# Prompt-chunk filler matmuls of a hybrid decoder step: six of eight weight tiles as three products of rounded halves

## The reference

```python
h = rms_norm(x, norm_mix)
u = h @ w_in                                  # RWKV part, attention part (q, k, v, f), gates
o_r = rwkv_time_mix(u_r, ...)                 # a delta-rule state, scanned over the rows
o_f = attend(q, k, v, log_sigmoid(f + b))     # softmax attention with forget bias
merged = sigmoid(g_r) * (o_r @ w_br_rwkv) + sigmoid(g_f) * (o_f @ w_br_fox)
x = x + merged @ w_out
x = x + square(relu(rms_norm(x) @ w_ffn_up)) @ w_ffn_down
```

## Time and profile before

| | us |
|---|---|
| median of 3 runs | 2157.71 (2157.24 to 2160.13) |
| the profiled execution's own time | 2151.56 |
| its span, first to last instruction | 2149.6 |
| TensorE busy | 2072.9 (96%) |
| VectorE busy | 908.4 (42%) |
| ScalarE busy | 597.7 (28%) |
| GpSimd busy | 191.8 (9%) |
| first fillers to the end of chunk 9 | 221 to 854 |

### The profile page before, as it was taken

The page is one execution under the profiler, slowest core; times in us unless marked ns, Lnnn a source line. Parts: engine busy times, 40 slices in busy tenths (PEclk is TensorE's granted clock), DMA queues, the critical chain, the costliest instruction groups (busy, mean ns, idle before and its releaser), DMA issues.

```text
span 2149.6 us, 42585 instructions
## 1 busy us (share of the span) xinstructions
PE 2072.9 (96%) x17394; PEld 1795.7 (84%) x17394; DVE 908.4 (42%) x1468; ACT 597.7 (28%) x963; POOL 191.8 (9%) x186
## 2 busy tenths in 40 slices
PE   7999999999999999999999999999999999999997
PEld 7996677777777777655566899999999999999997
DVE  6557444433444442505776654432222213212334
ACT  5015222221222222213544642332012102202213
POOL 0000222122222212001110000000000000000000
PEclk9999999999999999999999999999999999999999
DMA  4204421101222111764745461111111111111112
GB/s 166 88 30 174 149 49 41 48 22 40 49 60 69 49 45 55 186 137 157 251 134 204 150 236 60 49 39 49 49 39 49 47 41 49 40 48 49 39 49 81
DMA packets 107238, 181.05 MB, mean 84 GB/s; under 512 B 60014, under 2 KB 63406, under 8 KB 105542
## 3 DMA queue, kind: packets, MB, share of 16 engines
q1 hardware_dynamic: 104806, 170.65, 25.2%
q10 hardware_dynamic: 2304, 8.50, 1.6%
HBM read 145.58 MB, written 33.54 MB: 83 GB/s over the span
## 4 chain that ended last, share of the span: by engine, by line
PE 70%; issue 17%; POOL 4%; DVE 3%; DMA 3%; SPq 1%; ACT 1%; POOLq 0%; ACTq 0%; DVEq 0%
PE ps L289 41%; PE ps L369 13%; PE ps L946 3%; POOL arena L2194 3%; PE ps L947 3%; DMA weights<-in_wu 1%; PE ps L1262 1%; DVE arena L1953 1%; PE ps L1128 1%; PE ps L1065 1%; PE ps L1187 1%; PE ps L1246 1%; DVE arena L1972 1%; DMA normed<-in_kp 1%; PE ps L1058 1%
## 5 line engine op out<-in xcount | busy, mean ns | idle before, releaser
L369 PE MATMUL ps<-normed,weights 128*128 128x350 f32 x1344 | 432.1, 469 | 0.8 <-ACT arena L382 0.6
L369 PEld LDWEIGHTS ps<-normed,weights 128*128 128x128 f32 x1344 | 246.6, 191 | 128.1 <-issue 7.3
L289 PE MATMUL ps<-h_high,wb_split 128*128 128x350 f32 x1536 | 290.5, 324 | 0.0
L289 PE MATMUL ps<-ff_high,wb_split 128*128 128x350 f32 x1488 | 281.0, 323 | 0.0
L299 ACT CAST wb_split<-weights 128x1024 fp32r<-128x1024 f32 x88 | 92.1, 1047 | 599.8 <-PE ps L289 591.9
L289 PEld LDWEIGHTS ps<-h_high,wb_split 128*128 128x128 f32 x1536 | 254.7, 189 | 0.4
L289 PEld LDWEIGHTS ps<-ff_high,wb_split 128*128 128x128 f32 x1488 | 247.2, 189 | 0.0
L2111 DVE TENSOR_TENSOR arena<-arena,ps 128x1050 f32 (+1 forms) x39 | 48.7, 1249 | 314.0 <-PE ps L289 314.0
L946 PEld LDWEIGHTS ps<-arena 64*64 64x64 f32 x2400 | 145.0, 135 | 26.5 <-issue 26.5
L2194 POOL TENSOR_TENSOR arena<-arena,constants 64x512 f32<-64x512 f32 x120 | 132.5, 1104 | 386.7 <-DVE arena L1803 325.2
L289 PE MATMUL ps<-ff_low,wb_split 128*128 128x350 f32 x744 | 160.3, 323 | 0.0
(11 more groups left out here) (305 smaller groups left out, 2863.4 us busy)
## 6 DMA issues: line engine op xcount, KB each, us to landing
weights<-in_wu SPq DMA_DIRECT2D x122, 512.0 KB, 3.5
normed<-in_vp SPq DMA_DIRECT2D x64, 260.0 KB, 4.4
normed<-in_kp SPq DMA_DIRECT2D x64, 256.0 KB, 5.3
arena<-chunk_dram SPq DMA_DIRECT2D x10, 1248.0 KB, 6.9
arena<-gate_dram SPq DMA_DIRECT2D x16, 525.0 KB, 4.0
chunk_dram<-arena SPq DMA_DIRECT2D x12, 520.0 KB, 5.3
chunk_dram<-fox SPq DMA_DIRECT2D x12, 520.0 KB, 4.6
arena<-samp_dram SPq DMA_DIRECT2D x10, 512.0 KB, 10.2
```

The lines of the kernel that those rows point to most:

```text
L289: last = pe.matmul(PS[:, 3 * s + g, 0:G], ws[s][wh][:, k * P:(k + 1) * P], tile_of(x[xh], k)[:, g * G:(g + 1) * G], start=(k == 0 and wh + ...
L369: last = self.pe.matmul(PS[:, 6 + m % 2, 0:G], W[:, s, k * P:(k + 1) * P], HT[:, k, g * G:(g + 1) * G], start=(k == 0), stop=(k == KT - 1))
```

## The change

The kernel's fillers of chunks 1 to 9 do the tiles k = 0 to 5 as three float32r products, the tiles 6 and 7 as before in float32. The order within a sub-unit becomes 6, 7, 0, ..., 5. For this:

- In chunk 0 ScalarE rounds six tiles of `HT` into `HF` (one behind each level's copies). After chunk 0 VectorE writes the low halves in place over the six tiles, `HL` (same memory as `HT`), 128x1050 each, and the first fillers of chunk 1 wait for them (`hl_made`). After chunk 9 it adds the halves back (`h_restored`); the first fillers after the chunks wait for that, and so does ScalarE before it writes `f_t`.
- The weights of a slot are split in each chunk: slot 1 in the chunk itself (ScalarE behind the copy `nat_k`, VectorE behind `nat_v`, ahead of the masks, in two parts of 512 and 256 columns), slot 0 of the next pair in the chunk before (ScalarE behind level 5, VectorE behind the levels). The low half is written in place over `W`.
- To make room, the low-rank gate goes to DRAM (`bg_dram` doubled, four more stores of 520 KB before chunk 0) and comes back with the bonus, so each chunk's load has twice the bytes; and four buffers share memory with others (`E2` with `Lm`, `NU` with `T1`, `Yc` with `Xm`; `gst` moves).
- Chunks 0 and 9 stand outside the loops of VectorE and ScalarE; otherwise the chunks are as before.

```diff
-                self.left = [(s, g, k) for s in range(2) for g in range(NG) for k in range(KT)]
+                late = [*range(NS, KT), *range(NS)] if ns or first else range(KT)
+                self.left = [(s, g, i, k) for s in range(2) for g in range(NG) for i, k in enumerate(late)]
...
+                        if g == 0 and self.ns:
+                            self.pe.wait_ge(wf_done[s], self.v - V_FOX0)
...
+                    if m == 0 and self.first is not None and k < NS:
+                        self.pe.wait_ge(self.first, k + 1)
+                    out, w = PS[:, 6 + m % 2, 0:G], W[:, s, k * P:(k + 1) * P]
+                    if k < self.ns:
+                        wl_ = WL[:, s, k * P:(k + 1) * P]
+                        self.pe.matmul(out, fill_w(s, k), HF[:, k, at], start=False, stop=False)
+                        self.pe.matmul(out, fill_w(s, k), HL[:, k, at], start=False, stop=False)
+                        last = self.pe.matmul(out, wl_, HF[:, k, at], start=False, stop=(i == KT - 1))
+                    else:
+                        last = self.pe.matmul(out, w, HT[:, k, at], start=(i == 0), stop=(i == KT - 1))
...
+        def fill_split_high(act, i, s):
+            act.wait_ge(w_in[s], 16 * i + 16 * (V_FOX0 + 1))
+            for k0, k1, t in WF[s]:
+                last = act.copy(t, W[:, s, k0 * P:k1 * P])
+            last.then_inc(wf_high[s], 1)
+        def fill_split_low(dve, i, s):
+            dve.wait_ge(wf_high[s], i)
+            for k0, k1, t in WF[s]:
+                last = dve.tensor_tensor(WL[:, s, k0 * P:k1 * P], W[:, s, k0 * P:k1 * P], t, ALU.subtract)
+            last.then_inc(wf_done[s], 1)
...
+            for p in range(HP):
+                sp.wait_ge(gt_read, NG * (p + 1))
+                sp.dma_start(bg_dram[:, HP + p, :], GT[:, p, 0:TP]).then_inc(bg_stored, 16)
...
-                fill = Filler(pe, c + V_FOX0) if c else fill0
+                fill = Filler(pe, c + V_FOX0, NS, hl_made if c == 1 else None) if c else fill0
...
-            Filler(pe, V_GATE0 + (NC - C_FOX)).run()
+            Filler(pe, V_GATE0 + (NC - C_FOX), first=h_restored).run()
...
                 ch_act.done(act.copy(Kn[0:C], PS[0:C, 0, :]), "nat_k")
+                if early:
+                    fill_split_high(act, c, 1)
...
+                    if lv == 5 and late:
+                        fill_split_high(act, c + 1, 0)
+                    if not early:
+                        if lv == 1:
+                            act.wait_ge(bg_stored, 16 * 2 * HP)
+                        act.copy(HF[:, lv - 1], HT[:, lv - 1, :]).then_inc(hf_made, 1)
...
+            act.wait_ge(h_restored, NS)
             order(act.activation(f_t[0:NH], lfT[0:NH], ACT.Abs))
...
                 done(dve.tensor_copy(Vn[0:C], PS[0:C, 3, :]), "nat_v")
+                if early:
+                    fill_split_low(dve, c, 1)
...
+                if late:
+                    fill_split_low(dve, c + 1, 0)
...
+            dve_chunk(0, early=False)
+            dve.wait_ge(hf_made, NS)
+            dve.wait_ge(unit_done, 2 * V_FOX0 + 2)
+            for k in range(NS):
+                dve.tensor_tensor(HL[:, k], HT[:, k, :], HF[:, k], ALU.subtract).then_inc(hl_made, 1)
+            with dve.Fori(1, NC - 1) as c:
+                dve_chunk(c)
+            dve_chunk(NC - 1, late=False)
+            dve.wait_ge(unit_done, 2 * (V_FOX0 + NC - 1) + 2)
+            for k in range(NS):
+                dve.tensor_tensor(HT[:, k, :], HL[:, k].bitcast(F32), HF[:, k].bitcast(F32), ALU.add)\
+                   .then_inc(h_restored, 1)
...
-                ch_pool.done(pool.tensor_tensor(here, here, GT[:, :, bass.ds(c * C, C)], ALU.mult), "gate")
+                ch_pool.done(pool.tensor_tensor(here, here, BGc[:, HP:2 * HP], ALU.mult), "gate")
```

More of the change, by code:

```diff
@@ L83 @@
 C_FOX = PV_FOX
+NS = 6
 SB_COLS = 56904
@@ L159, in build @@
         cst = keep_tensor("constants", C_ALL)
+        w_at = placed
         W = keep_tensor("weights", 2, D)
@@ L162, in build @@
         wl = keep_tensor("lora_weights", 512)
+        wg_at = placed
         wg = keep_tensor("gate_weights", 512)
@@ L354, in build, with __init__ @@
         class Filler:
-            def __init__(self, pe, v):
-                self.pe, self.v = pe, v
-                self.left = [(s, g, k) for s in range(2) for g in range(NG) for k in range(KT)]
+            def __init__(self, pe, v, ns=0, first=None):
+                self.pe, self.v, self.ns, self.first = pe, v, ns, first
+                late = [*range(NS, KT), *range(NS)] if ns or first else range(KT)
+                self.left = [(s, g, i, k) for s in range(2) for g in range(NG) for i, k in enumerate(late)]
             def run(self, n=None):
-                for s, g, k in self.left[:n]:
+                for s, g, i, k in self.left[:n]:
                     m = NG * s + g
-                    if k == 0:
-                        if g == 0:
+                    at = slice(g * G, (g + 1) * G)
+                    if i == 0:
+                        if g == 0 and self.ns:
+                            self.pe.wait_ge(wf_done[s], self.v - V_FOX0)
+                        elif g == 0:
                             self.pe.wait_ge(w_in[s], 16 * self.v + 16)
                         self.pe.wait_ge(sub_read, 2 * NG * self.v + (m + 1 - 2 * NG * V_FOX0))
-                    last = self.pe.matmul(PS[:, 6 + m % 2, 0:G], W[:, s, k * P:(k + 1) * P],
-                                          HT[:, k, g * G:(g + 1) * G], start=(k == 0), stop=(k == KT - 1))
-                    if k == KT - 1:
+                    if m == 0 and self.first is not None and k < NS:
[8 more added lines that the diff above has]
+                        last = self.pe.matmul(out, w, HT[:, k, at], start=(i == 0), stop=(i == KT - 1))
+                    if i == KT - 1:
                         last.then_inc(unit_done if g == NG - 1 else sub_done, 1)
@@ L520, in build @@
         Lc, Lm = r_ch.take(HP, C), r_ch.take(HP, C)
-        E1, E2, E3 = r_ch.take(HP, C), r_ch.take(HP, C), r_ch.take(HP, C)
+        E1, E2, E3 = r_ch.take(HP, C), Lm, r_ch.take(HP, C)
         AR = r_ch.take(HP, 2, C)
         Kc, Bc, Vc = r_ch.take(HP, C), r_ch.take(HP, C), r_ch.take(HP, C)
-        Kn, Bn, Vn = r_ch.take(512), r_ch.take(512), r_ch.take(512)
+        Kn, BGc, Bn, Vn = r_ch.take(512), r_ch.take(2 * HP, C), r_ch.take(512), r_ch.take(512)
         HB, HR = 64, C - 64
@@ L534, in build, with fill_w @@
         Zm = r_c2.take(512)
-        NU = r_c2.take(512)
+        NU = T1.rearrange("p a b -> p (a b)")
+        Yc = Xm.rearrange("p a b -> p (a b)")
+        gst = r_c2.take(4, NH)
         St = r_ch.take(HP, HD)
[L537 to L540, removed]
+        hf_at = -(-r_ch.at // 8) * 8
+        HF = own("fill_high", hf_at, NS, TT, dtype=F32R)
+        HL = own("fill_low", ht_at, KT, TT, dtype=F32R)
+        wf_at = hf_at + -(-NS * TT // 8) * 8
+        WF = [[(0, NS, own("w_fill0", wf_at, NS * P, dtype=F32R))],
+              [(0, 4, own("w_fill1a", wg_at, 4 * P, dtype=F32R)),
+               (4, NS, own("w_fill1b", wf_at + NS * P, (NS - 4) * P, dtype=F32R))]]
+        WL = own("w_fill_low", w_at, 2, D, dtype=F32R)
+        assert r_ch.at <= GT_at and wf_at + (2 * NS - 4) * P <= ar_end
+        wf_high, wf_done = [sem("wf_high0"), sem("wf_high1")], [sem("wf_done0"), sem("wf_done1")]
+        hf_made, hl_made, h_restored = sem("hf_made"), sem("hl_made"), sem("h_restored")
+        def fill_w(s, k):
+            return [t[:, (k - k0) * P:(k - k0 + 1) * P] for k0, k1, t in WF[s] if k0 <= k < k1][0]
+        def fill_split_high(act, i, s):
[8 more added lines that the diff above has]
+            last.then_inc(wf_done[s], 1)
         bonus_added = sem("bonus_added")
@@ L1441, in gate_out, with act_chunk @@
                 act_fill(act, x + V_GATE0, m, SGs[:, s, g * G:(g + 1) * G])
-            def act_chunk(c, gates):
+            def act_chunk(c, gates, early=True, late=True):
                 def out(m):
@@ L1504, in act_chunk @@
                                                bias=par[:, V_LB + p:V_LB + p + 1]), f"y_{p}")
-            with act.Fori(0, C_FOX) as c:
+            act_chunk(0, False, early=False)
+            with act.Fori(1, C_FOX) as c:
                 act_chunk(c, False)
-            with act.Fori(C_FOX, NC) as c:
+            with act.Fori(C_FOX, NC - 1) as c:
                 act_chunk(c, True)
+            act_chunk(NC - 1, True, late=False)
             act.wait_ge(ch_pe.sem, ch_pe.before(NC))
@@ L1773, in _, with dve_chunk @@
             dve.sem_inc(ch_dve.sem, 1)
-            with dve.Fori(0, NC) as c:
+            def dve_chunk(c, early=True, late=True):
                 def wait(steps, name):
@@ L2200, in _ @@
                 here = YT[:, :, bass.ds(c * C, C)]
-                ch_pool.done(pool.tensor_tensor(here, here, BGc, ALU.add), "bonus")
+                ch_pool.done(pool.tensor_tensor(here, here, BGc[:, 0:HP], ALU.add), "bonus")
```

(2 more changed lines are left out.)

4 lines of the change are left out of this document (2 added, 2 removed).

## The result

The changed kernel took 2140.2 us in the median of six executions (2131.3 to 2144.5), beside 2156.1 (2149.4 to 2160.1) of the kernel before; the ratio is 0.993, interval [0.9906, 0.9955]. The forecast was 2144.1, within 2134 to 2154. The gain of the medians is 15.8 us against 13.6 forecast.

A forecast was written before the change was run, and what follows sets the result against it. TensorE was taken to bound the kernel, VectorE only in the mask steps. 34.4 - 10.6 - 7.5 - 1.0 = 15.3, less 1.7 for one clock fall, gives 13.6: 2157.7 - 13.6 = 2144.1 us, range 2134 to 2154.

The forecast's parts named there:

- Fillers: TensorE's fillers in chunks 1 to 9: each of 324 split products saves 0.106 us, 34.4 us if every place stays covered.
- the third rival: Split fillers: weight loads set the pace, about 0.19 us a step; 12 us slower, 2170 us; chance 0.06.
- The covers: Places where TensorE arrives later than what it waits for, as before y_back: shorter fillers bring no new wait; margins 0.4 to 0.9.
- The second rival: A cover fails: slot 1's high half late or y_back waits for the norm; some 1 us a chunk, 2153; chance 0.08.
- Slot 1's low half: Two VectorE subtractions ahead of the masks make TensorE idle 1.18 us more a chunk; 10.6 us in nine chunks.
- The lower value from the time per column: Alternative size of slot 1's low half ahead of the masks, from the 1050-column step: 0.9 us instead of 1.18.
- Chunk 0 to 1: Six subtractions after chunk 0's norm delay chunk 1 by 4.5 us; lost saving 1.3, clock fall 1.7; together 7.5, bounds 3 to 11.
- Behind chunk 9: After the last chunk: 0.6 us of split-product saving lost to the norm wait, 0.4 for restoring six tiles; 1.0, bounds 0 to 4.
- The gate and the buffers: Four more gate stores before chunk 0, twice the bonus bytes and shared buffers add no wait: nothing.
- From the profiled execution to the median: The median was put 6.15 us above the profiled execution, a difference the change doesn't touch.
- The falls: Rival: TensorE's clock falls in the mask steps of most chunks, 1.7 us each, nine 15.3, gain 0, 2157.8; chance 0.17.
- more is seen: Case: low half partly absorbed, no fall of the clock at all; gain 20 to 24 us, 2134 to 2138; chance 0.05.

The follow-up runs named there:

- after_again: The changed kernel run once more without any edit, beside the kernel before; 2134.9 us, ratio 0.9924.
- both: Changed kernel with slot 1's low half moved behind xt_init and two unsplit filler products moved into TensorE's wait for the first mask; 2119.4 us, ratio 0.9849.
- no_switch: gap_fill without the six subtractions after chunk 0, six additions after chunk 9 and their waits; low product reads the high half; 2114.4 us, ratio 0.9806.
- gap_fill: Changed kernel with two unsplit filler products moved from behind z into TensorE's wait for the first mask; 2118.9 us, ratio 0.9849.
- before_wait: Kernel before plus two VectorE subtractions of constants into unread memory, between the copy of v and the first mask; 2166.7 us, ratio 1.0068.

## Why the prediction came out right, step by step

The stretch that the change touches reaches from the norm of chunk 0 to the last y_back. In the kernel before it takes 853.96 - 287.66 = 566.3 us; in after_again 832.53 - 286.20 = 546.3, a gain of 20.0; in the first profile, with its eight falls, 846.86 - 287.21 = 559.65, a gain of 6.65. My terms up to that point were 34.4 - 10.6 - 7.5 - 0.6 = 15.7.

- *Fillers, 34.4.* Right: 0.107 us a product where 0.106 was computed, 34.6 in nine chunks. The step of 0.161 held in blocks of six between other shapes, so the third rival, that the weight load sets the pace, is out.
- *The covers.* Right: y_back still starts by TensorE's own end behind chunks 0 to 8, and its row names no wait; the subtractions of slot 1 come right behind the copy of v, so ScalarE's half was in time. The second rival is out.
- *Slot 1's low half, 10.6.* Mis-sized. The mechanism is as put, but it is 0.92 to 0.94 us a chunk, 8.4 in all. I added recorded durations and gaps; the steps follow each other faster than they last. The lower value from the time per column (0.9) was named and not taken. TensorE's wait came out as 1.55 us for the same reason, not 1.9.
- *Chunk 0 to 1, 7.5.* Right within its bounds: 7.1. The pieces, in the changed kernel, then in both, the one kernel with the switch and all split products whose profile has no fall there:

```profile
287.21 0.69 DVE L1927 TENSOR_TENSOR arena<-arena 104x512 f32<-104x512 f32 x1 [1.96 <-ACT arena L1551]
287.93 7.88 DVE L1933 TENSOR_TENSOR fill_low<-normed,fill_high 128x1050 fp32r<-128x1050 f32 x6
...
303.31 0.69 DVE L1853 COPY arena<-ps 104x512 f32<-104x512 f32 x1 [1.78 <-PE ps L976]
```

```profile
285.65 0.69 DVE L1929 TENSOR_TENSOR arena<-arena 104x512 f32<-104x512 f32 x1 [1.96 <-ACT arena L1553]
...
300.10 0.69 DVE L1855 COPY arena<-ps 104x512 f32<-104x512 f32 x1
```

  Six subtractions of 1.25 us at a step of 1.16, one of them slowed by GpSimd to 2.06, and the copy of b 16.1 us behind the norm's start. The forecast was 15.3 (303.0 - 287.66) and the 1.7 of a fall on top of it. In both it is 14.45, in no_switch 9.3: so up to the copy of b 5.2 us are the switch, where 4.5 + 1.3 = 5.8 was put, and 1.6 the fall. The clock fell there in both profiles of the changed kernel. The sign given for it, chunk 1 longer than chunk 2 by about 7.5, was badly chosen: from y_back to y_back chunk 1 takes 355.62 - 290.99 = 64.63, only 4.8 more than 59.80, as a part of the cost stands ahead of the first y_back.
- *Behind chunk 9, 1.0.* 1.1, in another split: the last chunk's gain is 61.48 - 59.42 = 2.06 where the others have 3.04, so 0.98 is not realised (0.6 forecast), and the restore costs 0.13 (0.4 forecast): from the last y_back to the transposes of v it is 886.76 - 853.96 = 32.80 in the kernel before and 879.79 - 846.86 = 32.93 in the changed one. The two rows, of before and of after:

```profile
886.76 1.04 PE L1099 MATMUL ps<-constants,fox 128*104 128x128 f32 x8
```

```profile
879.79 1.03 PE L1145 MATMUL ps<-constants,fox 128*104 128x128 f32 x8
```

- *The gate and the buffers, nothing.* 0.12 us a chunk, some 1.1 in all, in favour, and not to be measured in the time. With it the measured terms make 34.6 - 8.4 - 7.1 - 1.0 + 1.1 = 19.2 of the 20.0; 0.8 us is not assigned.
- *From the profiled execution to the median.* I added 6.15 us as the kernel before had it in three executions. Its medians with more executions were 2156.1 and 2151.4 to 2151.8, so this offset was a matter of those three; the ratios are what compares.
- *The falls.* Here the case was wrongly cut. I gave them 0.17 as a rival that holds or doesn't, and took one fall for the rest. By the times they came in seven of twelve executions, but only the two profiles show it, with eight and none. The price of a fall was right (1.65). In the execution without them the gain is 2151.56 - 2128.89 = 22.7, the 20 to 24 of "more is seen"; with them it is 7.1. The Trainium skill's page TensorE: Matmul & The Clock Gate, section "HAM oscillation", has a loop that idles in the same place of every turn, for some 3 to 5 us, pay in every turn; here, at 1.55 us, one profile agrees and the other does not, with the same code and the same wait.

So the mechanism of the gain was right, and that the number came out so near is in part luck: errors against each other. Up to the last y_back and without falls my terms were 20.0 - 15.7 = 4.3 us short, of which 2.2 are the low half put too dear and 1.1 the gate not seen. Against that, I took 1.7 for falls, where they cost 13.2 in the profile that has them. And the 6.15 added for the median did not show in the later groups. The median of the first six, 2140.2, belongs to the upper group, between 2139.2 and 2144.5; of the second six three were in the lower, and their median, 2134.9, is 9.2 below the forecast. The period by which I called the forecast wrong, above 61.5, was missed by 0.05 us in the profile with falls.

## What to carry to other kernels

Put work that only a later step needs behind the last instruction that the pacing engine waits for: the two subtractions cost 0.93 us a chunk ahead of the masks and nothing behind xt_init, where they even take more than twice as long. Where an engine waits in the same place of every turn, move filler work into the wait: here two moved products gave 1.16 us a chunk, 10.5 in nine, and no fall stood in chunks 2 to 9 of that profile. By its median gap_fill took 16 to 21 us less than the changed kernel (2134.9 and 2140.2); that the rest of this is falls that no longer come is likely, not shown. And split a gain into what the change needs and what the kernel before could have had: 10.8 of 33 us here were open without it.

## What the runs showed of the hardware

- One kernel, with the same 1.55 us wait in each turn, had eight clock falls 61.4 us apart in one profile and none in that stretch in another; its times lie in two groups, 2139 to 2144 us and 2129 to 2133. In before_wait, whose wait is 1.66, five turns of seven had one.
- A fall to 1.2 GHz cost 1.65 us (changed kernel) and 1.64 us (before_wait) a turn.
- Two VectorE steps of 0.69 and 0.42 us took 0.94 us of the engine's time, start to start.
- A two-input step of 512 columns took 0.69 us alone and 1.65 beside GpSimd's, one of 256 columns 0.42 and 1.09.
- Three float32r products with new weights each took 0.482 us at 350 columns, one float32 product 0.588, and 36 such replacements changed the period by 3.85 us, where 36 times the difference is 3.8.
